# One matrix of an MoE weight stream, split between SyncE's queue and small GpSimd loads

## The reference, cut to what matters

```python
for e in range(N_EXPERTS):                       # 32
    gate = jnp.minimum(hf @ w_gate[e] + b_gate[e], SWIGLU_LIMIT)
    up = jnp.clip(hf @ w_up[e] + b_up[e], -SWIGLU_LIMIT, SWIGLU_LIMIT)
    act = gate * jax.nn.sigmoid(SWIGLU_ALPHA * gate) * (up + 1.0)
    y = y + combine[:, e:e + 1] * (act @ w_down[e] + b_down[e])
```

## Time and profile before

| | |
|---|---|
| median of 3 runs | 1166.69 us (1166.63 to 1167.01) |
| the profiled execution's own time | 1165.3 us |
| its span, first to last instruction | 1163.5 us |
| TensorE busy | 1120.5 us (96%) |
| bytes moved by DMA | 445.52 MB, mean 383 GB/s |
| mean granted clock of TensorE | 0.985 |

### The profile page before, as it was taken

The page is one execution under the profiler, slowest core; times in us unless marked ns, Lnnn a source line. Parts: engine busy times, 40 slices in busy tenths (PEclk is TensorE's granted clock), DMA queues, the critical chain, the costliest instruction groups (busy, mean ns, idle before and its releaser), DMA issues.

```text
span 1163.5 us, 15045 instructions
## 1 busy us (share of the span) xinstructions
PE 1120.5 (96%) x6121; PEld 559.2 (48%) x6121; DVE 368.0 (32%) x895; ACT 256.5 (22%) x528; POOL 15.6 (1%) x20
## 2 busy tenths in 40 slices
PE   9999999999999999898989899999999998999998
PEld 8998989864343434242424233323343433443333
DVE  5477765641223122112121212121212121222213
ACT  6466554430111111011111111111110111110102
POOL 1000000000000000000000000000000000000000
PEclk9999999999999999999999989998999998999999
DMA  9856567799999999999999999999999999999995
GB/s 286 275 173 187 166 211 275 298 364 408 416 428 424 432 431 430 431 431 431 431 429 430 432 431 431 431 431 432 431 432 432 432 431 429 428 428 428 422 422 227
DMA packets 53069, 445.52 MB, mean 383 GB/s; under 512 B 3746, under 2 KB 32088, under 8 KB 35984
## 3 DMA queue, kind: packets, MB, share of 16 engines
q1 hardware_dynamic: 50954, 439.83, 91.3%
q0 software_dynamic: 1248, 4.20, 1.3%
q10 hardware_dynamic: 806, 0.59, 0.2%
HBM read 443.47 MB, written 1.13 MB: 382 GB/s over the span
## 4 chain that ended last, share of the span: by engine, by line
PE 67%; DMA 28%; DVE 2%; issue 1%; ACT 1%; SPq 1%; ACTq 0%; DVEq 0%
PE psum L1372 25%; DMA ring<-in_w_up 24%; PE psum L1401 13%; PE psum L1295 5%; PE psum L995 4%; PE psum L996 4%; PE psum L997 4%; PE psum L1310 4%; DMA ring<-in_w_down 3%; PE psum L1318 2%; PE psum L1042 1%; PE psum L1135 1%; SPq L551 1%; PE psum L1111 1%; ACT high L748 1%
## 5 line engine op out<-in xcount | busy, mean ns | idle before, releaser
L1372 PE MATMUL psum<-ring,xT 128*64 128x512 f32 x960 | 436.0, 611 | 35.5 <-DMA ring<-in_w_up 34.9
L1373 PE MATMUL psum<-ring,xT 128*64 128x512 f32 x960 | 436.1, 611 | 0.0
L1372 PEld LDWEIGHTS psum<-ring,xT 128*64 128x64 f32 x960 | 132.2, 140 | 315.3 <-issue 276.5
L1401 PE MATMUL psum<-ring,guT 128*64 128x512 f32 x984 | 224.5, 598 | 0.4 <-DVE guT L1871 0.4
L1852 DVE COPY gu<-psum 128x512 f32<-128x512 f32 x32 | 33.5, 1046 | 573.9 <-PE psum L1373 573.9
L1373 PEld LDWEIGHTS psum<-ring,xT 128*64 128x64 f32 x960 | 132.2, 140 | 0.0
L1401 PEld LDWEIGHTS psum<-ring,guT 128*64 128x64 f32 x984 | 65.2, 136 | 134.2 <-issue 111.4
L935 ACT COPY gu<-psum 128x512 f32<-128x512 f32 x32 | 34.0, 1061 | 419.1 <-PE psum L1373 419.1
L1540 DVE TENSOR_TENSOR low<-raw,high 128x2048 fp32r<-128x2048 f32 x31 | 71.1, 2297 | 37.3 <-ACT high L748 37.3
L995 PE MATMUL psum<-hT_hi,high 128*128 128x256 f32 x272 | 78.3, 288 | 0.1
L996 PE MATMUL psum<-hT_lo,high 128*128 128x256 f32 x272 | 76.9, 283 | 0.0
(11 more groups left out here) (210 smaller groups left out, 1026.8 us busy)
## 6 DMA issues: line engine op xcount, KB each, us to landing
ring<-in_w_down SPq DMA_DIRECT2D x25, 4096.0 KB, 20.8
ring<-in_w_up SPq DMA_DIRECT2D x24, 4096.0 KB, 29.3
ring<-in_w_gate SPq DMA_DIRECT2D x23, 4096.0 KB, 30.1
ring<-in_w_up SPq DMA_DIRECT2D x14, 2048.0 KB, 11.9
ring<-in_w_gate SPq DMA_DIRECT2D x12, 2048.0 KB, 19.8
raw<-in_w_in SPq DMA_DIRECT2D x22, 1024.0 KB, 5.4
ring<-in_w_down SPq DMA_DIRECT2D x7, 2048.0 KB, 12.9
ring<-in_w_down SPq DMA_DIRECT2D x12, 1024.0 KB, 19.4
```

What stands on the lines that cost most here:

```text
L1372: mm(every(bank(GU + nb)[0:CAP, :]), x_k, of_chunks(gate[:, k, :], nb), start=k == 0, stop=k == KC - 1)
L1373: done = mm(every(bank(GU + nb)[CAP:P, :]), x_k, of_chunks(up[:, k, :], nb), start=k == 0, stop=k == KC - 1)
L1401: done = mm(o[half * CAP:(half + 1) * CAP, :], values[:, k, :], chunk_k[:, half * BANK:(half + 1) * BANK], start=k == 0, stop=k == KC - 1)
```

## The change

The down matrix of expert 12 (m = 38, the name `LEAN`) no longer comes in one load of 4096 KB. SP loads the chunks 4 to 7 of the partitions 0 to 63 (1 MB) and then all chunks of the partitions 64 to 127 (2 MB). The chunks 0 to 3 of the partitions 0 to 63 (1 MB) are loaded by GpSimd, in eight loads of eight partitions, 128 KB each, one row of 16 KB for each partition. Ahead of each stands a load of 128 bytes into a new small tile, `turnstile` (8 partitions of 16 bytes). GpSimd waits for the same release of the place as SP. TensorE waits for both semaphores, `place_in` and the new `lean_in`, and GpSimd waits for its small loads at the end. In a further pass SP would load the 1 MB itself.

```diff
+LEAN, LEAN_ROWS, LEAN_STEP = 3 * 12 + 2, P // 2, 8
...
+        turnstile = place("turnstile", [LEAN_STEP, LEAN_ROWS // LEAN_STEP, 4])
...
+        lean_in, turned = sem("lean_in"), sem("turned")
...
-            return sum(SPLITS[k] if k < len(SPLITS) else not by_parts(k) for k in range(m % RING, m + 1, RING))
+            return sum(SPLITS[k] if k < len(SPLITS) else 2 if k == LEAN else not by_parts(k)
+                       for k in range(m % RING, m + 1, RING))
...
                 for m in range(3 * RING, TAIL):
-                    if not by_parts(m):
+                    if m == LEAN:
+
+                        free(m, 1)
+                        e, kind = MATRICES[m]
+                        low_rows, high_rows = slice(0, LEAN_ROWS), slice(LEAN_ROWS, P)
+                        sp.dma_start(ring[m % RING][low_rows, HALF:, :].rearrange("p c n -> p (c n)"),
+                                     weights_of[kind][e][low_rows, HALF:, :].rearrange("p c n -> p (c n)")
+                                     ).then_inc(place_in[m % RING], 16)
+                        if not first:
+                            sp.dma_start(ring[m % RING][low_rows, 0:HALF, :].rearrange("p c n -> p (c n)"),
+                                         weights_of[kind][e][low_rows, 0:HALF, :].rearrange("p c n -> p (c n)")
+                                         ).then_inc(lean_in, 16)
+                        sp.dma_start(ring[m % RING][high_rows, :, :].rearrange("p c n -> p (c n)"),
+                                     weights_of[kind][e][high_rows, :, :].rearrange("p c n -> p (c n)")
+                                     ).then_inc(place_in[m % RING], 16)
+                    elif not by_parts(m):
                         free(m, 1)
                         load(m, 0, KC, place_in[m % RING])
...
+            e, kind = MATRICES[LEAN]
+            pool.wait_ge(used, released(LEAN - RING, PARTS - 1))
+            for i in range(LEAN_ROWS // LEAN_STEP):
+                pool.dma_start(turnstile[:, i, :], io["norm_final"][4 * LEAN_STEP * i:4 * LEAN_STEP * (i + 1)]
+                               .rearrange("(p n) -> p n", n=4)).then_inc(turned, 16)
+                r = slice(i * LEAN_STEP, (i + 1) * LEAN_STEP)
+                pool.dma_start(ring[LEAN % RING][r, 0:HALF, :].rearrange("p c n -> p (c n)"),
+                               io[("w_gate", "w_up", "w_down")[kind]][0][e].rearrange("(p c) n -> p c n", c=KC)
+                               [r, 0:HALF, :].rearrange("p c n -> p (c n)")).then_inc(lean_in, 16)
+            pool.wait_ge(turned, 16 * (LEAN_ROWS // LEAN_STEP))
...
                 pe.wait_ge(place_in[i], 16 * (p * in_pass(i) + in_place(m)))
+                if m == LEAN:
+                    pe.wait_ge(lean_in, 16 * p + 16 * (LEAN_ROWS // LEAN_STEP))
```

## The result

The changed kernel takes 1191.79 us (median of 6 runs, 1189.21 to 1194.82), the kernel before 1166.38 us on the same chip (6 runs, 1165.15 to 1167.01). The ratio is 1.0222, with an interval of 1.0211 to 1.0232: 25.9 us slower, where 7.4 were forecast and 1179.2 us was the upper end of the range. The profiled execution has a span of 1190.0 us.

The account below looks back on a forecast made before the run. The prediction took the always-busy DMA engines' byte stream as the bound; 0.1 (small loads) - 2.4 (relief) + 9.7 (narrow loads) = +7.4 us gave 1174.1 us against the runs' median, range 1164.2 to 1179.2.

Parts of the forecast that it names:

- The frame: Whole kernel: DMA engines always busy, so time lost before about 1136 us moves the end by as much.
- The narrow term: Expert 12's down matrix: 4 MB in loads into few partitions cost 9.7 us more, bounds 0 to 15.6.
- A narrow byte takes the time of two: Factor of 1 for loads into few partitions, taken from three dips in the earlier trace; gave 9.7 us.
- The estimate from the Trainium skill: Same 4.19 MB, priced at 196 GB/s for 64 partitions: 21.4 us in place of 9.7, 11.7 us more.
- The narrowest loads: GpSimd's eight-row loads hold their engines, at 27 GB/s for a load: +12 to +16 us, chance 0.12.
- Two of the signs: Signs of held engines: deeper dip, lasting past 620 us, and TensorE's wait near 611 us growing over 12 us.
- The cover step: At expert 12's down matrix: it lands 7 us before TensorE needs it, so less lateness holds up nobody there.
- the same lateness of the stream and not one more: TensorE's second wait costs 0, at worst the matrix's lateness beyond 7 us, already counted in the stream.
- The small loads at 0.1 us: GpSimd's eight 128-byte loads ahead of its large ones: 1 KB in all, set at 0.1 us.
- The relief of 2.4 us: GpSimd's 1 MB falls only on the eight engines that are ahead: -2.4 us, bounds -2.4 to +2.4.
- the late eight: Eight DMA engines supposed to carry all instruction packets, 112 KB more each, so 4.2 us behind at the end.
- the first rival: Narrow loads cost nothing and the right eight engines are relieved: -2.3 us, 1164.4 us, chance 0.28.

Follow-up runs that it names:

- e5: Kernel before, with SP loading the matrix as two 2 MB loads, even partitions and odd partitions, nothing from GpSimd: ratio 1.0000, cost 0 us.
- e1: The change with SP issuing all three pieces (low 1 MB, low 1 MB, high 2 MB) and GpSimd none of it: ratio 1.0113, +13.2 us over the kernel before.
- e6: Kernel before, with SP loading 2 MB into all partitions, then 1 MB each into the low and high halves: ratio 1.0064, +7.5 us.
- e18: SP loads odd partitions and half the even ones' chunks; GpSimd's 1 MB in two loads, even partitions of each half: ratio 1.0046, +5.4 us over the kernel before.
- e14: As e11, but GpSimd's 1 MB in four loads of 16 rows, every eighth partition: ratio 1.0048, +5.6 us over the kernel before.
- e11: The change spread over all partitions, without small loads; GpSimd's eight loads take every fourth partition in blocks of 32: ratio 1.0055, +6.4 us over the kernel before.
- e15: As e11, with all loads on SP's queue and nothing from GpSimd: ratio 1.0068, +7.9 us over the kernel before.
- e12: Kernel before, with SP loading the matrix in four 1 MB loads of 32 neighbouring partitions: ratio 1.0122, +14.2 us.
- e9: The change without its eight small loads, all else the same: ratio 1.0189, +22.0 us over the kernel before.
- e13: The change without small loads and with GpSimd's 1 MB as one load of partitions 0 to 63: ratio 1.0131, +15.3 us over the kernel before.
- e2: Kernel before, matrix whole from SP, plus 16 GpSimd loads of 128 bytes that TensorE waits for: ratio 1.0018, +2.1 us.
- e7: Kernel before plus 512 KB nobody waits for, in eight GpSimd loads of eight rows, each behind a small load: ratio 1.0016, +1.9 us.
- e8: As e7, but each eight-row load stands ahead of its small load: ratio 1.0014, +1.6 us over the kernel before.

## Why the prediction was wrong

**Right.** The frame: a full stream, in which every loss at 575 us stands at the end. In each run the loss by the windows and the cost agree within 3.5 us (the loss is that of one execution). SP's second issue and the split of the matrix cost nothing (e5). The sign, the place, the dip at a share near 1, and the software queue's bytes came as forecast.

**The narrow term was mis-sized, 9.7 us for 13.2.** "A narrow byte takes the time of two" fits the rate while such loads are under way (about half, in e1 as in e6), but not the whole cost. About 3 us or more come on top, whatever the size: 1 MB costs 5.4 to 7.9 us (e18, e14, e11, e15), 2 MB 7.5 (e6), 4 MB 13.2 (e1), while the rule gives 2.4, 4.9 and 9.7. Each cost has an interval of about 2 us to either side, so the 3 us are rough; what they are is open. The estimate from the Trainium skill, page "SBUF — State Buffer", section "Door 1: The DMA port swizzle", was 11.7 us; e1 with 13.2 is nearer to it than to 9.7. What made the rule right was not the count of partitions, which I had from the dips of the earlier trace rows, but where the partitions lie (e5, e12).

**The narrowest loads were put in as a rival, and it came true on top.** The step is "I take 9.7, between the three, though the eight-row loads are narrower than any row". It priced GpSimd's 1 MB like the other 3. Beyond the halves, eight neighbouring rows cost 6.7 us more (e9 minus e13). I had priced them by 27 GB/s for eight partitions, 12 to 16 us, but as something that happens in place of the forecast, with a chance of 0.12; and I ended the range there. Two of the signs that I had given for it came: a dip until past 620 us, and a wait longer by more than 12 us. Both mechanisms act together: 13.2 + 6.7 is 20 of the 22.0 us of e9.

**The cover step failed.** "That is the cover: a matrix late by less than 7 us holds up nobody at that place" was worked out for one load of SP's, and it holds for the kernel before (that load landed after 19.1 us, not the 20.8 of the median). GpSimd's last eight-row load was issued at 579.3, sooner than I had it, and landed at 635.8, 34 us after TensorE had come to the matrix. I had said that the lateness of the matrix is "the same lateness of the stream and not one more". It is one more when the wait is long: while TensorE stands, no place comes free, SP issues nothing for 47 us and the queue runs dry from 655 to 665 us, 5.5 us of the loss by the windows. In e9, where the wait was 10.63 us, the queue didn't run dry. The net of both, the change against e9, is 3.9 us; by themselves, late small loads and the gap that they bring cost 2.1 us (e2).

**The small loads at 0.1 us.** Their bytes are nothing; their way through the queue is not. In e2 they are late by themselves and cost 2.1 us, in the change 3.9.

**The relief of 2.4 us was not found.** e7 and e8 don't differ beyond their intervals, and no kernel here is faster than before. The term was also too large by its own numbers: with the others 2.4 us later and the late eight 4.2 us behind before, the last engine ends 4.2 - 2.4 = 1.8 us earlier and not 2.4. (The lower end of the range, 1164.2, should for its part be the 1164.4 of the first rival.) Whether the late eight engines exist isn't shown by any run.

Taken step by step from e1 over e13 and e9 to the change, the sum is 13.2 (halves, e1) + 2.1 (GpSimd issues one of them, e13 less e1, which may be 0) + 6.7 (eight neighbours) + 3.9 (small loads) = 25.9 us. Each term is the difference of two runs in a row, so the sum has to close; what it shows is the share of each.

## What to carry to other kernels

In a stream that fills the DMA engines, look at which partitions a load writes, not at how many: loads of 1 MB into 32 or 64 neighbours, or into one half, took the whole stream to about half its rate while they were under way, and every eighth of all 128 cost as much, while every second or every fourth partition of all 128 cost nothing. A mechanism for which no row exists is to be priced as a term of the sum as long as it can act beside the others. And a load that others must wait for is judged by its landing in the full queue, not by its bytes: when the reader stands, the ring gives no place and the stream can dry up later.

## What the runs showed of the hardware that was not expected

- Loads of 128 bytes from GpSimd beside a full stream of SP took up to 54.1 us to land in the change; in e2, with the stream at its full rate, TensorE could go on only 31 us after the last of them was issued. The profile doesn't show what holds them.
- The rate with 32 neighbouring partitions to a load is that with 64: 210 GB/s from 580 to 600 us in e12 and 193 to 229 in e1, at a share of 0.94 to 1.09.
- Loads into the low and into the high half don't make up for each other: in e12 SP issued two of each within 2 us, and the stream stayed at half rate for some 25 us.
